# Stick-breaking attention summed by parts, and chunked attention's bias and maximum in one VectorE operation

## The reference, cut to what matters

```python
# A: softmax over a band of chunks
scores = q @ k.T * dh**-0.5 + bias          # bias from a table of relative positions
out_a  = softmax(scores) @ v
# B: for each query, over the keys before it
z         = q @ k.T * dh**-0.5
log_keep  = where(causal, -softplus(z), 0.0)
log_after = cumsum(log_keep, reverse=True) - log_keep
w         = where(causal, exp(log_sigmoid(z) + log_after), 0.0)
out_b     = w @ v
```

## Time and profile before

| what | value |
|---|---|
| median of three runs | 3213.13 us (3210.9 to 3216.05) |
| the profiled execution's own time | 3212.68 us |
| its span, first to last instruction | 3210.8 us |
| mean granted TensorE clock | 0.983 of full speed |
| PE busy over the span | 3082.9 us (96%) |
| DVE busy | 2305.5 us (72%) |
| ACT busy | 1303.1 us (41%) |
| POOL busy | 807.8 us (25%) |
| att2, branch A | about 2073.6 to 2181.5 us of the span |
| att2, branch B | about 2181.5 to 2363.5 us |

### The profile page before, as it was taken

The page is one execution under the profiler, slowest core; times in us unless marked ns, Lnnn a source line. Parts: engine busy times, 40 slices in busy tenths (PEclk is TensorE's granted clock), DMA queues, the critical chain, the costliest instruction groups (busy, mean ns, idle before and its releaser), DMA issues.

```text
span 3210.8 us, 37676 instructions
## 1 busy us (share of the span) xinstructions
PE 3082.9 (96%) x14546; PEld 2417.3 (75%) x14546; DVE 2305.5 (72%) x3084; ACT 1303.1 (41%) x2124; POOL 807.8 (25%) x831
## 2 busy tenths in 40 slices
PE   7999998999999899999999999998899989999999
PEld 3577876777887788888877888764567877888787
DVE  6654456975657977778888566686644699899896
ACT  5431114761134433344454323476632344444443
POOL 1211101321120443320002444313533124333101
PEclk9999999999999999999999999999999999999999
DMA  6433352206743222246343346521123422222823
GB/s 223 156 133 132 136 206 102 80 14 236 266 142 116 99 86 86 80 150 226 112 135 112 97 124 202 174 99 39 39 89 113 156 86 85 79 85 73 298 89 112
DMA packets 118299, 406.86 MB, mean 127 GB/s; under 512 B 13704, under 2 KB 16328, under 8 KB 113642
## 3 DMA queue, kind: packets, MB, share of 16 engines
q1 hardware_dynamic: 65626, 200.42, 19.7%
q0 software_dynamic: 52496, 204.04, 17.7%
HBM read 321.50 MB, written 82.90 MB: 126 GB/s over the span
## 4 chain that ended last, share of the span: by engine, by line
PE 80%; DVE 11%; issue 3%; ACT 3%; DMA 2%; POOL 1%; SPq 0%; ACTq 0%; DVEq 0%; POOLq 0%
PE PS L455 23%; PE PS L457 23%; PE PS L456 23%; PE PS L1255 2%; PE PS L1295 2%; DVE HL L411 2%; PE PS L3447 2%; PE PS L1285 1%; PE PS L3469 1%; DMA RAW<-in_w_whyp 1%; POOL Sc L3702 1%; PE PS L3486 1%; ACT HL L393 1%; DVE Xp L1110 1%; DVE H L750 0%
## 5 line engine op out<-in xcount | busy, mean ns | idle before, releaser
L455 PE MATMUL PS<-H,HL 128*128 128x512 f32 x1920 | 761.1, 396 | 14.5 <-DVE H L3754 7.2
L456 PE MATMUL PS<-H,HL 128*128 128x512 f32 x1920 | 752.1, 392 | 0.0
L457 PE MATMUL PS<-H,HL 128*128 128x512 f32 x1920 | 752.0, 392 | 0.0
L393 ACT ACTIVATE HL<-RAW 128x512 fp32r<-128x512 f32 (+1 forms) x429 | 312.0, 728 | 619.6 <-PE PS L457 562.0
L411 DVE TENSOR_TENSOR HL<-RAW,HL 128x512 fp32r<-128x512 f32 (+1 forms) x429 | 400.1, 933 | 145.2 <-ACT HL L393 135.8
L455 PEld LDWEIGHTS PS<-H,HL 128*128 128x128 f32 x1920 | 363.2, 189 | 104.1 <-issue 19.3
L456 PEld LDWEIGHTS PS<-H,HL 128*128 128x128 f32 x1920 | 363.3, 189 | 76.9 <-issue 2.6
L457 PEld LDWEIGHTS PS<-H,HL 128*128 128x128 f32 x1920 | 363.1, 189 | 76.8
L455 PE MATMUL PS<-HT,HL 128*128 128x512 f32 x720 | 282.5, 392 | 17.8 <-DVE rows L2410 15.7
L456 PE MATMUL PS<-HT,HL 128*128 128x512 f32 x720 | 281.6, 391 | 0.0
L457 PE MATMUL PS<-HT,HL 128*128 128x512 f32 x720 | 281.4, 391 | 0.0
(11 more groups left out here) (465 smaller groups left out, 5633.0 us busy)
## 6 DMA issues: line engine op xcount, KB each, us to landing
RAW<-in_w_up SPq DMA_DIRECT2D x100, 512.0 KB, 3.6
RAW<-in_w_down SPq DMA_DIRECT2D x82, 512.0 KB, 3.8
RAW<-in_w_proj SPq DMA_DIRECT2D x48, 512.0 KB, 3.6
scr_hid<-hidr POOLq DMA_DIRECT2D x36, 512.0 KB, 2.9
RAW<-in_w_wmodr SPq DMA_DIRECT2D x32, 512.0 KB, 4.5
HL<-in_w_dfwd POOLq DMA_DIRECT2D x16, 1024.0 KB, 6.8
HL<-in_w_dinv POOLq DMA_DIRECT2D x16, 1024.0 KB, 5.4
RAW<-in_w_wout SPq DMA_DIRECT2D x26, 512.0 KB, 4.4
```

Of the source, the lines that this page charges most:

```text
L393: e.activation(part_slot(k, p)[0], src, ACT.Copy).then_inc(*k.high.mark(j, x))
L455: e.matmul(out, lh, rh, start=first, stop=False, skip_group_check=goes_on)
L456: e.matmul(out, lh, rl, start=False, stop=False, skip_group_check=goes_on)
L457: return e.matmul(out, ll, rh, start=False, stop=last, skip_group_check=goes_on)
```

## The change

In branch A, the addition of the bias and the row maximum become one instruction, `tensor_tensor_reduce`: it writes the negated biased scores and their minimum (which is the negated maximum), and the exponential takes them with `scale=-1.0`. The scores' PSUM bank is released by this one instruction. DVE now evicts every second turned group of A, and ACT the others.

In branch B, the sum is made by parts. Since the weight is P(j+1) - P(j), the sum of weights times values is the sum over j of P(j) (v(j-1) - v(j)), plus the last value. So PE turns the products P straight from `E2`; there is no take, no second sigmoid and no multiplication on POOL. The values are replaced by their steps v(j-1) - v(j). Two transfers for each pair of heads (`load_steps`) bring the values moved down by one row into a free slot of `Sc`, and two DVE instructions of 1024 columns (`steps`) subtract the values from them: `d` holds the steps of every row, and `v2` is overwritten with the steps in which the last row of each block has the value added back, for the block on the diagonal. So the value sum of a group of B uses two sets of values; its diagonal block is split in two 128-column parts, and one more matmul for each head is made for a group; the columns are as many as before. ACT evicts all turned blocks of B. The scores' bank is released after keep. DVE makes the steps in iteration u = 30, 38, 46 and 54, ahead of `low` and `left` in that iteration. POOL issues the loads in u = 26, 34, 42 and 50, behind those of `load_pair`.

```diff
@@ turns_att2
-                unit.append((heads, c, w, 4 + n % 2, "dve" if br and len(unit) % 2 else "act"))
+                unit.append((heads, c, w, 4 + n % 2, "dve" if br == 0 and len(unit) % 2 else "act"))
@@ value_sums
+    if br:
+        left, right = slice(0, 128), slice(128, 256)
+        if t == 0:
+            return [(0, left, True, True, True), (0, right, False, True, False), (1, right, True, False, True)]
+        return ([(kb, slice(0, 256), False, kb == 0, False) for kb in range(t)]
+                + [(t, left, True, False, True), (t, right, False, False, False), (t + 1, right, True, False, True)])
@@
+def v_steps(k, p):
+
+    return k.Sc[:, 5 * (1 - p % 2), :].rearrange("p (t n) -> p t n", t=8)
@@ pe_att2
-                free[b] = [s.dve.at("biased", u, hh) if br == 0 else s.act.at("take", u, hh)]
+                free[b] = [s.dve.at("max", u, hh) if br == 0 else s.act.at("keep", u, hh)]
@@
-                e.wait_ge(*(s.act.at("exp", u, hh) if br == 0 else s.pool.at("w", u, hh)))
-                src = k.E2 if br == 0 else k.Sc
+                e.wait_ge(*(s.act.at("exp", u, hh) if br == 0 else s.dve.at("left", u, hh)))
@@
+            if br:
+                e.wait_ge(*s.dve.at("steps", p, 1))
             claim(b)
-        for i, (kb, cols) in list(enumerate(sums))[m * half:m + m * half]:
+        for kb, cols, whole, first, last in sums[m:] if half else sums[:m]:
+            v = k.v2[:, pn % 2] if whole else v_steps(k, p)
@@ act_att2
-            e.activation(ev, ev, ACT.Exp, bias=st[:, sl, 0:1], accum_out=st[:, sl, 1:2]).then_inc(*s.act.mark("exp", u, hh))
+            e.activation(ev, ev, ACT.Exp, bias=st[:, sl, 0:1], scale=-1.0, accum_out=st[:, sl, 1:2]).then_inc(*s.act.mark("exp", u, hh))
@@
-        e.wait_ge(*s.dve.at("biased", NU // 2 - 1, 1))
-        e.activation(Sc[:, sl, 0:n], z, ACT.Sigmoid).then_inc(*s.act.mark("take", u, hh))
@@ dve_att2
-        e.tensor_tensor(ev, scores_of(k, u, hh), B[:, 2 * p + hh, 640 - n:640], ALU.add).then_inc(*s.dve.mark("biased", u, hh))
-        e.wait_ge(*s.dve.at("biased", u, hh))
-        e.tensor_reduce(st[:, sl, 0:1], ev, AX.X, ALU.max, negate=True).then_inc(*s.dve.mark("max", u, hh))
+        e.tensor_tensor_reduce(ev, scores_of(k, u, hh), B[:, 2 * p + hh, 640 - n:640], -1.0, 3.0e38, ALU.add, ALU.min,
+                               st[:, sl, 0:1]).then_inc(*s.dve.mark("max", u, hh))
@@
+    def steps(p):
+
+        v, d = k.v2[:, p % 2], v_steps(k, p)
+        e.wait_ge(*k.in_pair[p % 2].at(4 + p, 1))
+        e.wait_ge(*k.in_steps[p % 2].at(p, 1))
+        e.wait_ge(*s.pool.at("first", p))
+        e.tensor_tensor(d, d, v, ALU.subtract).then_inc(*s.dve.mark("steps", p, 0))
+        e.wait_ge(*s.dve.at("steps", p, 0))
+        e.scalar_tensor_tensor(v, v, k.ident[:, 127:128], d, ALU.mult, ALU.add).then_inc(*s.dve.mark("steps", p, 1))
@@
+        if u >= NU // 2 - 2 and u % 8 == 6 and u // 8 - 3 < 4:
+            steps(u // 8 - 3)
@@ pool side
+def load_steps(k, e, p):
+
+    s, d, src = k.att2, v_steps(k, p), k.d_v2[1][:, :, blk(p)].rearrange("t p n -> p t n")
+    if p == 1:
+        e.wait_ge(*s.dve.at("max", NU // 2 - 1, 1))
+    at = k.in_steps[p % 2]
+    e.memset(d[0:1, 0, :], 0.0).then_inc(*s.pool.mark("first", p))
+    e.dma_start(d[1:128], src[0:127]).then_inc(*at.mark(p, 0))
+    e.dma_start(d[0:1, 1:8], src[127:128, 0:7]).then_inc(*at.mark(p, 1))
@@ pool_att2
+            if u // 8 + 1 >= 4:
+                load_steps(k, e, u // 8 - 3)
-                e.wait_ge(*s.dve.at("left", u + 1, hh))
-                e.wait_ge(*s.act.at("take", u + 1, hh))
-                e.tensor_tensor(tk, tk, E[:, sl, 1:n], ALU.mult).then_inc(*s.pool.mark("w", u + 1, hh))
```

More of the change, by code:

```diff
@@ L3423, in value_sums @@
     br, p, t = UNITS[2 * g]
-    kbs = range(max(0, t - 4) if br == 0 else 0, t + 2)
-    cols = {kb: slice(128 if kb > t else 0, 128 if br == 0 and kb == t - 4 else 256) for kb in kbs}
-    return [(kb, cols[kb]) for kb in [t] + [kb for kb in kbs if kb != t]]
+    if br:
[4 more added lines that the diff above has]
+                + [(t, left, True, False, True), (t, right, False, False, False), (t + 1, right, True, False, True)])
+    kbs = range(max(0, t - 4), t + 2)
+    cols = {kb: slice(128 if kb > t else 0, 128 if kb == t - 4 else 256) for kb in kbs}
+    order = [t] + [kb for kb in kbs if kb != t]
+    return [(kb, cols[kb], True, kb == t, kb == order[-1]) for kb in order]
+def v_steps(k, p):
+    return k.Sc[:, 5 * (1 - p % 2), :].rearrange("p (t n) -> p t n", t=8)
 def pe_att2(k, e, free):
@@ L3465, in turn @@
             for i, hh in enumerate(heads):
-                e.wait_ge(*(s.act.at("exp", u, hh) if br == 0 else s.pool.at("w", u, hh)))
-                src = k.E2 if br == 0 else k.Sc
+                e.wait_ge(*(s.act.at("exp", u, hh) if br == 0 else s.dve.at("left", u, hh)))
                 for q in range(w):
-                    y = e.transpose(PS[:, b, blk(w * i + q)], src[:, slot(u, hh), blk(c + q)], k.ident[:, :])
+                    y = e.transpose(PS[:, b, blk(w * i + q)], k.E2[:, slot(u, hh), blk(c + q)], k.ident[:, :])
             y.then_inc(*s.pe.mark("turn", u, x))
@@ L3481, in values_of @@
                     e.wait_ge(*turned(k, u, x))
+            if br:
+                e.wait_ge(*s.dve.at("steps", p, 1))
             claim(b)
-        for i, (kb, cols) in list(enumerate(sums))[m * half:m + m * half]:
+        for kb, cols, whole, first, last in sums[m:] if half else sums[:m]:
+            v = k.v2[:, pn % 2] if whole else v_steps(k, p)
             for hh in range(2):
                 r = slice(64 * hh, 64 * hh + 64)
-                x = e.matmul(PS[r, b, cols], k.v2[:, pn % 2, kb, r], k.WT2[:, g % 2, hh, kb, cols], start=(i == 0), stop=(i == 2 * m - 1),
-                             skip_group_check=True)
+                x = e.matmul(PS[r, b, cols], v[:, kb, r], k.WT2[:, g % 2, hh, kb, cols], start=first, stop=last, skip_group_check=True)
         if half == 0:
@@ L3515, in act_att2 @@
     s, PS, H = k.att2, k.PS, k.H
-    st, E, Sc = k.st2, k.E2, k.Sc
+    st, E = k.st2, k.E2
     def exponents(u, hh):
@@ L3681, in load_queries @@
     e.dma_start(k.q2[:, g % 2, :], k.d_qk2[8 * br + p][:, blk(t // 2, 256)]).then_inc(*k.in_q[g % 2].mark(g))
+def load_steps(k, e, p):
[6 more added lines that the diff above has]
+    e.dma_start(d[0:1, 1:8], src[127:128, 0:7]).then_inc(*at.mark(p, 1))
 def pool_att2(k, e):
-    s, E, Sc = k.att2, k.E2, k.Sc
     for u in range(NU + 2):
@@ L3912, in build @@
         k.in_q = [dma(f"in_q{i}") for i in range(2)]
+        k.in_steps = [dma(f"in_steps{i}") for i in range(2)]
         k.in_gate = [dma(f"in_gate{i}") for i in range(4)]
```

## The result

The changed kernel takes 3284.56 us (median of four runs, 3282.62 to 3287.3) against 3212.02 before; the ratio is 1.0225, 95% interval 1.0207 to 1.0243. It is 72.5 us slower. The forecast was 3168. The profiled execution has a span of 3283.4 us at a mean clock of 0.969.

A forecast was written before the change was run, and what follows sets the result against it. PE was busy for 96% of the span, with B bound by waiting from engine to engine. A 9.8 + B 35.5 = 45.3 us off 3213.1 gave 3168 us, range 3154 to 3186.

The forecast's parts named there:

- the third rival: Branch B: DVE's steps wait for their loaded values, delaying scans and PE; slower, 3226 if landing 20 us later; chance 0.03.
- The fused operation: Branch A, DVE: bias and maximum in one instruction take 0.82 + 0.08 us at 640 columns.
- The bound from the scan: Branch A: upper bound for bias and maximum in one instruction, at the scan's rate, 1.48 + 0.08 us.
- rival 2: Branch A: bias and maximum in one run at the scan's rate, 1.56 us, so A gains nothing; 3178; chance 0.07.
- A was sized 9.8 us: Branch A: 7.3 us from PE's bank waits over four pairs plus 2.5 at the start; bounds 0 and 13.
- The banks' part: Branch A: PE waits less for PSUM banks inside 640-column scores, saving 1.8 us a pair, 7.3 for four.
- the start of A: First units of A: ten maxima, 5.5 us, stand in the unhidden chain; half saved, 2.5 us (bounds 1 and 5).
- B was sized 35.5 us: Branch B, four pairs: 11.5 + 8.1 + 7.8 + 8.1 us saved, bounds 20 and 47.
- Rival 1: Branch B stays bound by hand-overs between engines, 36.5 us a pair or more; 3183; chance 0.12.
- The steps were to cost nothing: Branch B: two DVE operations, about 2.5 us, fit in DVE's slack; cost 0, otherwise 2.5 us a pair.
- rival 4: End of the stage: the next stage waits for something else, so the change does nothing; 3213; chance 0.03.
- The port shared by DVE and POOL: First B pair: POOL's products slow scans to 3004 ns against 2276; nothing contests the port afterwards; counted in its 11.5 us.

The follow-up runs named there:

- 128 rows: Changed kernel with the shifted values loaded by one transfer of 128 partitions, from one row further up, first row zeroed on DVE: 3168.26 us.
- 122 partitions: Changed kernel with the 127-partition transfer cut in 122 and 5 partitions, the last row's transfer kept: 3195.07 us.
- the run by SP: Changed kernel with the same transfers of 127 partitions and of the last row issued by SP instead of POOL: 3226.37 us.
- the idle transfer: Kernel with the 128-partition load, plus a POOL-issued 127-partition transfer for pairs 1, 2 and 3 of B that no step waits for: 3261.34 us.

## Why the prediction was wrong

**The step that failed.** It is the third rival's, "a load of this size lands in 5.7, so 5.5 us are spare", by which the forecast put the wait in front of `steps` at nothing. I priced the load by its size, from a row with 128 partitions. This one has 127. POOL is kept from it for 4.3 to 5.4 us, takes 6.7 us to issue it, and DVE gets it 33.2 us after that issue began, 27.5 us later than rows 14 would have it. The spare time itself was right: with 128 rows DVE comes for the load 5.6 to 6.6 us after it has landed. The rival got 0.03 because "Nothing in the profile points there". None of the rows read from before shows a transfer of 127 partitions or any like number, so rows 14 were no bound for it, and I should have said that the price was open.

The rival's mechanism for DVE was right, and its threshold of 17 us fits the runs: with the load 12.4 us later than in rows 14 (122 partitions) the kernel still gains, with 25.0 us later and POOL's queue free (the run by SP) it loses. That the run by SP came out at 3226, the very price of the rival, is luck. The rival had its load 20 us late with 5.5 to spare, there it is 25 us late with 9 to spare.

**What I left out of it.** The rival lets only DVE's order be late. Fed with DVE's measured waits, 101.5 us in four places, its sum gives 3213.1 + 101.5 - 45.3 = 3269, which is 15 us short. POOL's order was as costly. `load_steps` is issued ahead of the queries of the next units, and those were in nobody's slack: PE needs them for the scores of the next pair. POOL's queue alone costs 28.5 us of PE's waiting a pair (the idle transfer), DVE's wait alone 15 in the run by SP and perhaps 24 as long as it is here. In the changed kernel they run side by side, and 26 to 30 us show, so a cure for one of them alone would not have saved the change. My table of slack had a row for the steps and none for the queries moved behind them.

**The sum of the loss.** The stage of the changed kernel is 362.4 - 246.8 = 115.6 us longer than with 128 rows. PE's four waits are 109.2 of them; the other 6 us are most likely the slow clock behind each wait (3.18 us for scores of 1.77), which no run here takes apart.

**What was right, seen with 128 rows.** The forecast of 3168 is met by the kernel with the load reshaped, 3168.26, in part by luck: the kernel before took 3209.92 beside it and not the 3213.1 that I started from, so the gain is 41.7 us in the medians and 43.0 in the stage, where 45.3 was forecast.

- The fused operation: 0.82 + 0.08 us forecast; 822 ns and 83 ns measured at 640 columns (the lines are of the changed kernel; with 128 rows it is 822 as well). The bound from the scan, and with it rival 2, is out.

```profile
L3613 DVE CUSTOM_DVE_ANT_0 E<-PS,Sc 128x640 f32<-128x640 f32 x32 | 25.1, 822 | 5.8 <-PE PS L3459 5.3
...
L3613 DVE DVE_READ_ACCUMULATOR2_ANT st<- 128x1 f32 x64 | 5.3, 83 | 0.0
```

- A's scores of 640 columns: forecast 1.35 us for t = 6 and 7, under 1.8 for t = 5. In the changed kernel, its last pair, t = 5, 6 and 7, to be read against the last three of the earlier trace rows:

```profile
2162.43 1.69 PE L3459 MATMUL PS<-k,q 64*128 64x512 f32 x8
2165.88 1.35 PE L3459 MATMUL PS<-k,q 64*128 64x512 f32 x8
2169.56 1.35 PE L3459 MATMUL PS<-k,q 64*128 64x512 f32 x8
```

- A was sized 9.8 us, and is 7.4 to 8.0: 7.4 from the trace (103.72 us to the first mask with 128 rows against 111.15), 8.0 by taking it out. The banks' part, forecast at 1.8 us a pair, was right (1.9 in the three scores shown above). What failed is the 2.5 us for the start of A: the first pair went from 25.3 us to 23.4, no more than a later one (28.3 to 26.2), so the start gave next to nothing.
- B was sized 35.5 us: the stretch from the first mask to the end is 143.1 us against 178.7, which is 35.6. A pair was to take 32.5 us, and takes 32.2 and 32.3. Rival 1 is out.
- The steps were to cost nothing. In the 128-row kernel no wait of DVE in front of them is left; the slack behind them is 1.5 us a pair and not 2 to 3.
- Gain passes to the end in full: the rest of the span is 2921 us before and after, and 2920 with 128 rows, so rival 4 is out.
- The port shared by DVE and POOL: the first pair's scans of 1024 columns, 3004 ns before, take 2274 with the products gone, though both operands are in SBUF still. That is what the others take (2268).

**The two sides of the sum.** Forecast gain 45.3 us; shown by the 128-row kernel 43.0 in the stage. What the change adds to that by its transfers is 115.6, and the difference, 72.6 in the stage, is the 72.5 of the result.

## What to carry to other kernels

A new transfer is priced by its outermost sizes and not by its bytes alone: see what divides them, and if the profile has no row of that shape, call its price open, or reshape it (here reading from one row further up turned 127 partitions into 128 and 116 us of waiting into none). Before a landing is read from a view, see how many transfers count on its semaphore; the wait of the engine that needs the data is the safer measure. When a step adds an issue to a queue, list what stands behind it there and when each of those is needed; the consumer of the new data may not be the first to be late. When a change comes out wrong by far more than any of its parts is worth, look for the one part that can be taken out or reshaped alone before the rest is judged: here nearly all the others were worth what the sum gave them.

## What the runs showed of the hardware

- One row decides: with 112 partitions (448 KB) in the large piece the load was there some 7.3 us after its issue began, with 113 (452 KB) after 30.4. With 122 (488 KB) it took 18.1, with 128 (512 KB) 6.6, with 127 (508 KB) 33.2. POOL's issue took 0.85, 6.0, 3.5, 0.89 and 6.7 us.
- With 1016 pieces in one transfer of 127 partitions POOL was kept from issuing for 4.3 to 5.4 us in front of it and for about 26 behind it; with 904, in 113 partitions, only once, for 1.4 us in front.
- Issued by SP the same transfer left POOL's loads alone, but DVE got it after 30.7 us and still waited for it, 16.2 us on average (64.9 in four).
- Two transfers on one semaphore can't be timed apart: the view gave 21.7 us to the large one of a load that was whole after 33.2; alone on a semaphore the same shape landed after 32.6.
- A scalar-tensor-tensor over two SBUF tensors took 1285 ns at 1024 columns, 60 more than the plain subtraction beside it (1224); the earlier trace rows had 1284 for 1023.
